# A mixture-of-experts tail: the last unit's outputs as a sixth tile of the way back, and a final norm by tile and half

## What is computed

```python
# h2: 256 tokens; each goes to 2 of 32 experts, ids sorted by expert
xs = xf[tok]
hg = ragged_dot(xs, w_gate, sizes); hu = ragged_dot(xs, w_up, sizes)     # 1024 -> 512
ys = ragged_dot(silu(hg) * hu, w_down, sizes)                            # 512 -> 1024
ys = ys * gates[order][:, None]
y = segment_sum(ys, tok, num_segments=t)      # back to the tokens
x = x + y
out = x * rsqrt(mean(x * x, -1) + 1e-6) * norm_f_w
```

## Time and profile before

| | us |
|---|---|
| median of 3 runs | 1124.17 |
| lowest, highest | 1121.33, 1125.53 |
| the profiled execution, its own time | 1122.43 |
| its span, first to last instruction | 1120.6 |
| TensorE busy / VectorE busy / ScalarE busy | 1053.4 / 840.5 / 660.6 |
| mean granted clock of TensorE | 0.979 |

### The profile page before, as it was taken

How to read it: one execution, slowest core, us unless ns; L and a number is a source line. 1 busy time by engine, 2 the same in 40 slices (tenths; PEclk the granted TensorE clock), 3 DMA queues, 4 the chain that set the end, 5 groups by cost and what they waited for, 6 DMA issues and landing times.

```text
span 1120.6 us, 15061 instructions
## 1 busy us (share of the span) xinstructions
PE 1053.4 (94%) x5674; PEld 894.4 (80%) x5674; DVE 840.5 (75%) x1072; ACT 660.6 (59%) x791; POOL 34.3 (3%) x40
## 2 busy tenths in 40 slices
PE   5999999999999899898987989999999999999984
PEld 5878999999999777798877868778778787787763
DVE  4755776666677556777657679999999999999964
ACT  4554655554456644455424567777777777777742
POOL 0000000000010100100020000000000000000000
PEclk9999999999999989999999989999999999999987
DMA  9633356556424533333203659899899899899940
GB/s 337 234 113 132 117 185 225 173 166 225 156 75 159 180 114 118 110 117 113 75 31 150 225 184 391 354 355 388 351 378 366 351 383 359 355 379 364 369 154 39
DMA packets 82565, 253.60 MB, mean 226 GB/s; under 512 B 4144, under 2 KB 42160, under 8 KB 62512
## 3 DMA queue, kind: packets, MB, share of 16 engines
q1 hardware_dynamic: 81664, 251.27, 60.3%
q10 hardware_dynamic: 816, 1.23, 0.3%
HBM read 251.44 MB, written 1.05 MB: 225 GB/s over the span
## 4 chain that ended last, share of the span: by engine, by line
PE 76%; DVE 10%; ACT 7%; issue 4%; POOL 1%; DMA 1%; DVEq 0%; POOLq 0%; SPq 0%; ACTq 0%
PE bank L1698 21%; PE bank L1700 21%; PE bank L1699 21%; PE bank L2165 4%; ACT WH L484 4%; DVE WL L915 3%; PE bank L2117 1%; DVE CV L1150 1%; PE bank L2147 1%; POOL sm L1658 1%; DMA cn<-in_cn 1%; PE bank L1724 1%; ACT HTH L503 1%; PE bank L2227 1%; ACT CV L491 1%
## 5 line engine op out<-in xcount | busy, mean ns | idle before, releaser
L915 DVE TENSOR_TENSOR WL<-raw,WH 128x2048 fp32r<-128x2048 f32 (+1 forms) x235 | 503.9, 2175 | 113.3 <-ACT WH L484 113.3
L484 ACT ACTIVATE WH<-raw 128x2048 fp32r<-128x2048 f32 (+1 forms) x235 | 427.1, 1824 | 105.3 <-PE bank L1700 94.0
L1698 PE MATMUL bank<-WH,MXH 128*128 128x512 f32 x552 | 220.3, 399 | 4.1 <-DVE MXL L1591 2.7
L1700 PE MATMUL bank<-WH,MXL 128*128 128x512 f32 x552 | 216.5, 392 | 0.0
L1699 PE MATMUL bank<-WL,MXH 128*128 128x512 f32 x552 | 216.2, 392 | 0.0
L1698 PE MATMUL bank<-HTH,WH 128*128 128x256 f32 x576 | 165.8, 288 | 3.5 <-DVE CV L1150 2.6
L1699 PE MATMUL bank<-HTL,WH 128*128 128x256 f32 x576 | 163.7, 284 | 0.0
L1700 PE MATMUL bank<-HTH,WL 128*128 128x256 f32 x576 | 163.6, 284 | 0.0
L1698 PE MATMUL bank<-WH,HTH 128*128 128x512 f32 x348 | 140.4, 403 | 7.4 <-DVE BIG L1574 4.2
L1699 PE MATMUL bank<-WL,HTH 128*128 128x512 f32 x348 | 137.6, 395 | 0.0
L1698 PEld LDWEIGHTS bank<-WH,MXH 128*128 128x128 f32 x552 | 104.9, 190 | 25.4 <-DVE MXL L1591 2.8
(11 more groups left out here) (342 smaller groups left out, 1114.1 us busy)
## 6 DMA issues: line engine op xcount, KB each, us to landing
raw<-in_exp_w_gate SPq DMA_DIRECT2D x52, 1024.0 KB, 8.0
raw<-in_exp_w_up SPq DMA_DIRECT2D x52, 1024.0 KB, 7.8
raw<-in_exp_w_down SPq DMA_DIRECT2D x52, 1024.0 KB, 5.6
raw<-in_w_in SPq DMA_DIRECT2D x34, 1024.0 KB, 5.3
raw<-in_w_up SPq DMA_DIRECT2D x22, 1024.0 KB, 5.2
raw<-in_w_down SPq DMA_DIRECT2D x11, 1024.0 KB, 5.3
raw<-in_w_out SPq DMA_DIRECT2D x8, 1024.0 KB, 5.1
raw<-in_w_o SPq DMA_DIRECT2D x4, 1024.0 KB, 5.3
```

Source lines behind the costliest of these rows:

```text
L484: e.activation(WH[i % HL][:, 0:n], raw[i % RAW][:, 0:n], ACT.Copy).then_inc(a_wh, 1)
L915: e.tensor_tensor(l, r, h.bitcast(F32), ALU.subtract).then_inc(v_wl, 1)
L1698: e.matmul(out_, ah, bh, start=start, stop=False)
L1700: return e.matmul(out_, al, bh, start=False, stop=stop)
```

## The change

- `last_unit` on ScalarE and VectorE does one split, turns the hidden values, and then does the second split; VectorE's gather of the unit before stands between.
- The last down products go to the banks of the next parity of `GU`, and are not gathered into YACC. They are two blocks of their own, (5, 0) and (5, 1), with a selection matrix that ScalarE copies from SELT at the unit's tile (`sel_last`, in the space of the router's weights).
- Twelve blocks go back: eight EARLY ones (five of the first half, three of the second), which ScalarE and VectorE make behind their second split, in the free piece of WH and WL and in MXH and MXL; and four LATE ones behind the down products, in the first down piece's space (`back_parts`). TensorE goes through all 24 matmuls of token tile 0, then those of tile 1, its first half first; `p_back` counts three stages. Banks are 5, 4, 6 and 7 (`SB`).
- The drains and the join are gone; the way back is part of `last_unit`, so it stands in each of its copies.
- Behind the units: the additions, the norm and the store of token tile 0 as soon as it is complete; of tile 1 the squares by half (two sums, added), the product with the weights ahead of the power, and the last scaling on ScalarE (first half) and VectorE (second half), with a store for each half.

Declarations of semaphores are left out.

```diff
--- before.py
+++ after.py
@@ -116,7 +116,7 @@
 A_CUM = numbered(["sel", "ident", "neg", "rows"])
 RSTD = numbered([(s, t) for s in ("mix", "attn", "ffn", "fin", "n1") for t in range(T)]
                 + ["ssd0", "ssd1", "ml0", "ml1"] + [(s, t) for s in ("n2", "out") for t in range(T)])
-SQ = numbered([(s, t) for s in ("mix", "ffn", "fin", "n1", "n2", "out") for t in range(T)])
+SQ = numbered([(s, t) for s in ("mix", "ffn", "fin", "n1", "n2") for t in range(T)] + [("out", i) for i in range(3)])
 V_ROUTE = numbered(["ge2", "mm", "dm", "h2l", "first", "units", "gates"])
 A_ROUTE = numbered(["h2h", "ge2", "dm"])
 P_ROUTE = numbered(["counts", "gates"])
@@ -127,6 +127,9 @@
 MIXB = [2, 3, 5, 7]
 SPB = {1: 0, 2: 4}
 GATB = [7, 0, 1, 2, 3, 4, 5, 6]
+SB = [[5, 4], [6, 7]]
+EARLY = [(j, 0) for j in range(NT)] + [(j, 1) for j in range(3)]
+LATE = [(NT, 0), (NT, 1), (3, 1), (4, 1)]
 X_COLS = numbered([(c, t) for c in range(2) for t in range(T)])
 X_ADDS = numbered([(n, t) for n in ("wm0", "wm1", "we0", "we1") for t in range(T)])
 FT0 = numbered([("up", g) for g in range(NG)] + [("xbc", c) for c in range(6)]
@@ -349,6 +352,19 @@
         SG = [cvf[:, i * 512:(i + 1) * 512] for i in range(2)]
         GU = [(0, 1), (2, 3)]
         TBK, YB = 4, (6, 7)
+
+        def back_parts(u, n):
+
+            i = unit_base(u + 1)
+            if n < 4:
+                v = WH[(i + 2) % HL], WL[(i + 2) % HL]
+            elif n < 8:
+                v = (w[:, :, :].rearrange("p a b -> p (a b)") for w in (MXH, MXL))
+            else:
+                v = WH[i % HL], WL[i % HL]
+            return [w[:, (n % 4) * 512:(n % 4 + 1) * 512] for w in v]
+
+        sel_last = wsh[:, 0:256]
         tri, ones = ux[:, 0:128], ux[:, 128:256]
 
         def heads4(v, t, g):
...
@@ -468,10 +483,13 @@
                 load_unit(u)
             more(LEAST)
 
-            for t in range(T):
-                e.wait_ge(v_fo, t + 1)
-                e.dma_start(out[t * P:(t + 1) * P, :], X[:, t, :]).then_inc(d_out, 16)
-            e.wait_ge(d_out, 16 * T)
+            e.wait_ge(v_fo, 1)
+            e.dma_start(out[0:P, :], X[:, 0, :]).then_inc(d_out, 16)
+            e.wait_ge(a_fo, 1)
+            e.dma_start(out[P:2 * P, 0:512], TMP[:, 0, :]).then_inc(d_out, 16)
+            e.wait_ge(v_fo, 2)
+            e.dma_start(out[P:2 * P, 512:1024], TMP[:, 1, :]).then_inc(d_out, 16)
+            e.wait_ge(d_out, 16 * 3)
 
         def scalar(e):
             own = Count(own_a)
@@ -878,9 +896,18 @@
                 split(i + 5)
 
             def last_unit(u):
-                split(unit_base(u + 1))
-                split(unit_base(u + 1) + 1)
+                i = unit_base(u + 1)
+                split(i)
                 turn_hidden(u)
+                split(i + 1)
+                e.activation(sel_last.unsqueeze(1), SELT[:, bass.ds(tile[u], 1), :], ACT.Copy).then_inc(a_selL, 1)
+                e.wait_ge(v_yg, 2 * u)
+                for n, (j, hf) in enumerate(EARLY):
+                    e.activation(back_parts(u, n)[0], YACC[hf][:, j, :], ACT.Copy).then_inc(a_yh, 1)
+                e.wait_ge(p_used, i + 2)
+                for n, (j, hf) in enumerate(LATE, 8):
+                    y = YACC[hf][:, j, :] if j < NT else bank[GU[(u + 1) % 2][hf]][:, :]
+                    e.activation(back_parts(u, n)[0], y, ACT.Copy).then_inc(a_yh, 1)
 
             def more(u):
                 with e.If(count > u):
@@ -895,15 +922,16 @@
             for u in range(1, LEAST):
                 unit(u)
             more(LEAST)
-            e.drain().then_inc(s_join, 1)
-            e.wait_ge(s_join, 3)
-
-            for j in range(NT):
-                for hf in range(2):
-                    i = 2 * j + hf
-                    e.activation(WH[i // 4][:, (i % 4) * 512:(i % 4 + 1) * 512], YACC[hf][:, j, :],
-                                 ACT.Copy).then_inc(a_yh, 1)
-            squares("out", (v_xadd, v_xadd), (10, 12))
+
+            e.wait_ge(v_xadd, 10)
+            e.activation(cvf, X[:, 0, :], ACT.Square, accum_out=ss[:, 0:1]).then_inc(a_sq, 1)
+            for hf in range(2):
+                e.wait_ge(v_xadd, 11 + hf)
+                e.activation(SG[hf], X[:, 1, hf * 512:(hf + 1) * 512], ACT.Square,
+                             accum_out=(ss, rs)[hf][:, 1:2]).then_inc(a_sq, 1)
+            e.wait_ge(v_xg, 2)
+            e.wait_ge(g_rstd, RSTD["out", 1])
+            e.activation(TMP[:, 0, :], TMP[:, 0, :], ACT.Copy, scale=rs[:, 1:2]).then_inc(a_fo, 1)
 
         def vector(e):
             own = Count(own_v)
@@ -1611,12 +1639,19 @@
             def last_unit(u):
                 i = unit_base(u + 1)
                 split(i)
-                split(i + 1)
                 turn_hidden(u)
                 e.wait_ge(p_used, unit_base(u) + 6)
                 gather_y(u - 1)
-                e.wait_ge(p_used, i + 2)
-                gather_y(u)
+                split(i + 1)
+                for n, (j, hf) in enumerate(EARLY):
+                    h, l = back_parts(u, n)
+                    e.wait_ge(a_yh, n + 1)
+                    e.tensor_tensor(l, YACC[hf][:, j, :], h.bitcast(F32), ALU.subtract).then_inc(v_yl, 1)
+                for n, (j, hf) in enumerate(LATE, 8):
+                    y = YACC[hf][:, j, :] if j < NT else bank[GU[(u + 1) % 2][hf]][:, :]
+                    h, l = back_parts(u, n)
+                    e.wait_ge(a_yh, n + 1)
+                    e.tensor_tensor(l, y, h.bitcast(F32), ALU.subtract).then_inc(v_yl, 1)
 
             def more(u):
                 with e.If(count > u):
@@ -1632,25 +1667,37 @@
             for u in range(1, LEAST):
                 unit(u)
             more(LEAST)
-            e.drain().then_inc(s_join, 1)
-            e.wait_ge(s_join, 3)
-
-            for j in range(NT):
-                for hf in range(2):
-                    i = 2 * j + hf
-                    e.wait_ge(a_yh, i + 1)
-                    h, l = (v[i // 4][:, (i % 4) * 512:(i % 4 + 1) * 512] for v in (WH, WL))
-                    e.tensor_tensor(l, YACC[hf][:, j, :], h.bitcast(F32), ALU.subtract).then_inc(v_yl, 1)
-            e.wait_ge(p_back, 1)
-            add_to_x((0, 1, 2, 3))
-            for t in range(T):
-                e.wait_ge(a_sq, SQ["out", t])
-                mean_eps(rs[:, t:t + 1], ss[:, t:t + 1], D).then_inc(v_ms, 1)
+
+            def add_back(t, hf):
+                xv = X[:, t, hf * 512:(hf + 1) * 512]
+                e.wait_ge(p_back, (1, 1, 2, 3)[2 * t + hf])
+                e.tensor_tensor(xv, bank[SB[t][hf]][:, :], xv, ALU.add).then_inc(v_xadd, 1)
+
+            def weighted(hf):
+                e.wait_ge(v_xadd, 11 + hf)
+                e.tensor_tensor(TMP[:, hf, :], X[:, 1, hf * 512:(hf + 1) * 512], gbf[:, hf * 512:(hf + 1) * 512],
+                                ALU.mult).then_inc(v_xg, 1)
+
+            add_back(0, 0)
+            add_back(0, 1)
+            e.wait_ge(a_sq, SQ["out", 0])
+            mean_eps(rs[:, 0:1], ss[:, 0:1], D).then_inc(v_ms, 1)
+            add_back(1, 0)
             e.wait_ge(d_gbf, 16)
-            for t in range(T):
-                e.wait_ge(g_rstd, RSTD["out", t])
-                e.scalar_tensor_tensor(out=X[:, t, :], in0=X[:, t, :], scalar=rs[:, t:t + 1], in1=gbf, op0=ALU.mult,
-                                       op1=ALU.mult).then_inc(v_fo, 1)
+            e.wait_ge(g_rstd, RSTD["out", 0])
+            e.scalar_tensor_tensor(out=X[:, 0, :], in0=X[:, 0, :], scalar=rs[:, 0:1], in1=gbf, op0=ALU.mult,
+                                   op1=ALU.mult).then_inc(v_fo, 1)
+            weighted(0)
+            e.wait_ge(a_sq, SQ["out", 1])
+            mean_eps(ss[:, 1:2], ss[:, 1:2], D).then_inc(own.up(), 1)
+            add_back(1, 1)
+            weighted(1)
+            e.wait_ge(a_sq, SQ["out", 2])
+            e.wait_ge(own.sem, own.n)
+            e.scalar_tensor_tensor(out=rs[:, 1:2], in0=rs[:, 1:2], scalar=1.0 / D, in1=ss[:, 1:2], op0=ALU.mult,
+                                   op1=ALU.add).then_inc(v_ms, 1)
+            e.wait_ge(g_rstd, RSTD["out", 1])
+            e.tensor_scalar(TMP[:, 1, :], TMP[:, 1, :], rs[:, 1:2], None, ALU.mult).then_inc(v_fo, 1)
 
         def gpsimd(e):
             def power(v, k):
@@ -2147,22 +2194,22 @@
                     m = e.transpose(bank[TBK][:, k * 128:(k + 1) * 128], SG[u % 2][:, k:512:4], ident)
                 m.then_inc(p_hidT, 1)
 
-            def down(u, i):
+            def down(u, i, banks=YB):
                 e.wait_ge(v_hil, u + 1)
                 for k in range(3):
                     if k % 2 == 0:
                         wh, wl = piece(i + k // 2, 2)
                     for hf in range(2):
                         hs = slice(hf * 512, (hf + 1) * 512)
-                        if k == 0 and u:
+                        if k == 0 and u and banks == YB:
                             e.wait_ge(v_yg, 2 * u - 1 + hf)
-                        m = three(bank[YB[hf]][:, :], HIH[u % 2][:, k, :], HIL[u % 2][:, k, :], wh[:, k % 2, hs],
```

(49 more changed lines are left out.)

## The result

| | before | changed |
|---|---|---|
| median, us | 1122.99 (4 runs) | 1108.89 (4 runs) |
| lowest to highest | 1121.33 to 1125.53 | 1107.42 to 1111.48 |
| span of the profiled execution | 1120.6 | 1105.6 |

The ratio is 0.9875, with a 95% interval of 0.9847 to 0.9903: faster, by 14 us in these runs. The changed kernel was measured again with the experiments: 1111.56 (6 runs, 1107.76 to 1113.86) against 1121.53, a ratio of 0.9913 (0.9894 to 0.9931). Over all ten executions its median is 1110.3, against 1122.2 for the 45 of before. So the gain is about 12 us, a little over 1%, and one kernel's executions are spread over 6 us.

The account below looks back on a forecast made before the run. It took TensorE, busy 94% of the span, as the bound, losing time in gaps, slow clock and the tail. Gains of 2.8, 0.8, 4.8, 0.9 and 1.8 sum to 11.1 us: 1113.0 on the median of 1124.17, range 1109 to 1118.

Parts of the forecast that it names:

- start of the down products: Last unit: with one split, turned values, then second split, the last down products begin at 1083.0, 2.8 us earlier.
- their length: Last down products: 7.45 us including one shorter clock fall, against 8.25 before, a gain of 0.8 us.
- the join's gap: Between down products and way back: the 4.8 us of last gather, drain, join, first copy and first difference goes.
- way back: TensorE's last matmuls: 48 instead of 40, at 0.23 us each, take 10.95 us against 11.8, a gain of 0.9.
- tail: Additions, norm and stores after TensorE's last matmul: 8.1 us instead of 9.9, a gain of 1.8.
- the term for POOL's power: In the tail's norm: POOL's power takes 1.66 us from the mean to the scaling, counted for each token tile.
- The clock in the down products: Behind the shortened gap of about 1.5 us, 8 or so matmuls run at 0.43 us, costing 1.0 us.
- full clock: Rival, chance 0.14: the 1.5 us gap ahead of the down products costs no clock; 1.0 us less, 1112.
- The cover of the eight differences: ScalarE's copies and VectorE's eight differences run beside the down products at no cost; without this cover, 4.9 us more.
- The exits: Jump out of the last unit's body: lower bound 1.7 us for VectorE, hidden; upper 5.4, 1115.6 (rival, chance 0.10).
- TensorE stood for no code inside the last unit: Against the slower rival, chance 0.03: code loading in the last unit, four waits of 5.4 us, gives 1134.6.
- never stayed at half clock: Against a rival, chance 0.05: waits for single blocks keep TensorE at half clock through the end, 1127 us.

Follow-up runs that it names:

- beside_power: The changed kernel with one more VectorE operation, two inputs in SBUF, beside POOL's last power: 27.05 us from the last transposes to the end, 0.98 more.
- no_overlap: The changed kernel with ScalarE's eight early copies held back until the last down products are through: 1113.62 us (4 runs), 0.9921 of before.

## Why the prediction was right or wrong

It said 1113.0 in 1109 to 1118, faster with 0.87. The sign and the mechanism hold. The first measurement lies 0.1 under the range; the second, 1111.56, inside. The forecast was 4.1 us too high. 1.2 of it was the base: the 1124.17 of three runs became 1122.99 with the fourth, and the 45 executions of before have 1122.2. The rest is the gain: the sum was 11.1 us; the stretch gives 13.65 from profile to profile (12.9 from the second profile of before), and the medians of all executions 11.8. Why the medians gained less than the stretch stays open; with ten executions spread over 6 us it may be chance in the part ahead. Term by term, in the profiled stretch:

| | predicted | measured |
|---|---|---|
| start of the down products | 2.8 | 2.9 |
| their length | 0.8 | 1.35 |
| the join's gap | 4.8 | 4.8 |
| way back | 0.9 | 0.9 |
| tail | 1.8 | 3.7 |

The join's 4.8 us, the largest term, is read from the two timelines; no run puts the join back by itself.

- **The step that failed is the tail, in the term for POOL's power.** I took 1.66 us from the second power of the earlier trace rows and used it twice. It is at most 0.73 for the first (1096.62 to 1097.35) and 0.72 for the second (1101.04 to 1101.76). The long one was no property of the operation: VectorE's scaling ran beside it, as beside_power showed. The new order has no such VectorE operation at either power. With the shorter first power the last addition isn't 0.85 late either, it starts 0.04 us behind TensorE. Together that is 1.75 of the 1.9 us by which the tail was mis-sized. The trace of before had a short power as well, 1.24 us ahead of the long one, and I gave no reason for taking the long one twice. The last store was issued 3.5 us behind TensorE's last matmul, not the 5 that the prediction named.
- **The clock in the down products** was the second one. I took one fall on the strength of the earlier trace rows, a gap of 1.43 us that had one behind it. None came in any of eight profiles of such a gap at this place: the rival "full clock" (0.14) was the right one, and the products took 6.9 us where the forecast had 7.45 and that rival 6.5. One row elsewhere was thin evidence: the same row came without a fall in six of 14 profiles. What decides it, and why 3.6 us didn't cost the clock here, stays open.
- **The part ahead of the change** was 1.36 us shorter in the profile after than in the profile of before, where its clock was lower (0.95 against 1.00 from 360 to 460). I had the spread of the three runs (4 us) before me, and let it reach down by only 1.7. The range's three terms in fact lead down to 1108.8, under the measured 1108.89, and were rounded to 1109. So by which side of the edge the first measurement fell is chance; that the sum was too small by the tail is not.
- The order of the splits starts the products 2.9 us earlier, but undoing it costs only 1.2 to 1.4 us: the products start 2.0 to 2.2 us later without it, but are then 0.8 us shorter, 0.53 of it the wait for piece two.
- The cover of the eight differences was real, and its price 3.7, not 4.9: TensorE takes the blocks as they come, so only the pace difference and the start count.
- The exits cost nothing, as the lower bound had it; no_overlap shows about 2 us for VectorE's, so SyncE's 5.4 us, the row that spoke for waiting on a fetch, were no measure of it. Whether the 2 us hold such a wait no run shows.
- TensorE stood for no code inside the last unit, never stayed at half clock, and no variant was slower than before.

## What to carry to other kernels

A gap on the busiest engine can cost more than its length, if the clock is slower behind it; here that second part was 3.4 to 4.2 us, about 30% of what the change gained in the stretch, and filler matmuls brought it back alone. But one row in which the clock fell behind a gap does not say that it will: ask more than one execution. When an operation appears in a trace with two durations, look at what the neighbour engine does beside it before putting either into a sum. And where executions differ by the clock in a part that the change doesn't touch, compare the stretch that it does.

## What the runs showed of the hardware

- POOL's power of one column takes 0.54 us; beside a VectorE operation of 1.28 us with two inputs in SBUF it takes 1.52, and ends 0.4 us behind it. In the kernel before it took 0.99 us (at 112.72) beside a VectorE tensor_scalar of 1024 columns and 0.74 us.
- The granted clock fell behind both gaps of 4.1 to 4.9 us in each of three profiles, and behind none of 3.6, 3.3, 1.6 and 1.3 to 1.4 us at the end of the kernel; yet it fell behind one and the same gap of 1.43 us at 396 in eight of 14 profiles.
- In no_overlap VectorE began the first operation behind the last unit's body 2.0 us after it began its last one inside (1101.5 to 1103.5), its input ready 0.5 us before; this is taken for the jump out.
